# First output projection: 16 modulation tiles from PE products to VectorE row sums; row transfers of the second input projection spread over more weight units

## The reference

```python
s_lat, s_ctx = silu(c), silu(c_ctx)
for l in range(2):                                   # first block
    shift, scale, gate = split(s_lat @ w_mod[l] + b_mod[l], 3)
    shift_c, scale_c, gate_c = split(s_ctx @ w_mod[l] + b_mod[l], 3)
    hx = rmsnorm(x, norm_g[l]) * (1 + scale) + shift       # 256 x 2048
    hc = rmsnorm(ctx, norm_g[l]) * (1 + scale_c) + shift_c
    y, y_c = mix(hx @ w_in[l], hc @ w_in[l], ...)          # attention, pooling, convolution
    if l == 0:
        ctx = ctx + gate_c * (y_c @ w_out[l])
    x = x + gate * (y @ w_out[l])
x = rmsnorm(x, final_g)
mod = silu(c_2) @ w_mod_2 + b_mod_2                  # second block, six parts
...
```

## Time and profile before

| | us |
|---|---|
| runs before, median of 3 | 3036.22 |
| lowest, highest | 3032.48, 3045.45 |
| the profiled execution | 3027.13 |
| its span, first to last instruction | 3025.4 |
| PE busy | 2879.7 (95%) |
| POOL busy | 1828.3 (60%) |
| DVE busy | 1689.8 (56%) |
| ACT busy | 1455.1 (48%) |
| transfers | 620.46 MB, 205 GB/s on average |

### The profile page before, as it was taken

The page is one execution under the profiler, slowest core; times in us unless marked ns, Lnnn a source line. Parts: engine busy times, 40 slices in busy tenths (PEclk is TensorE's granted clock), DMA queues, the critical chain, the costliest instruction groups (busy, mean ns, idle before and its releaser), DMA issues.

```text
span 3025.4 us, 49352 instructions
## 1 busy us (share of the span) xinstructions
PE 2879.7 (95%) x18353; PEld 2486.3 (82%) x18353; DVE 1689.8 (56%) x2879; ACT 1455.1 (48%) x2231; POOL 1828.3 (60%) x756
## 2 busy tenths in 40 slices
PE   7799999999889989999997999999999999999999
PEld 5688886777768888878877888899987888888888
DVE  2477972899533668247669999673324444442000
ACT  3222223556422432248645777675445555555443
POOL 1244443333233565445575677677887888888998
PEclk9999999999999999999998999999999999999999
DMA  9877322555676695233593444444555666765665
GB/s 397 320 264 274 137 97 97 184 193 202 256 271 244 249 396 230 97 105 112 183 348 130 151 154 152 147 147 159 186 191 173 239 238 223 245 215 193 206 208 187
DMA packets 148917, 620.46 MB, mean 205 GB/s; under 512 B 16512, under 2 KB 17840, under 8 KB 129840
## 3 DMA queue, kind: packets, MB, share of 16 engines
q1 hardware_dynamic: 147632, 613.44, 57.0%
q10 hardware_dynamic: 1152, 5.24, 0.5%
HBM read 616.49 MB, written 2.12 MB: 204 GB/s over the span
## 4 chain that ended last, share of the span: by engine, by line
issue 46%; POOL 29%; PE 23%; POOLq 1%; DVE 0%; DVEq 0%
POOL w_low L690 29%; PE bank L725 16%; PE bank L726 8%; POOLq L685 0%; POOLq L689 0%; POOLq L690 0%; DVE region L1866 0%; DVE region L1869 0%; DVEq L1866 0%; POOLq L2675 0%
## 5 line engine op out<-in xcount | busy, mean ns | idle before, releaser
L690 POOL TENSOR_TENSOR w_low<-raw,w_high 128x1024 fp32r<-128x1024 f32 x752 | 1828.1, 2448 | 1186.5 <-ACT w_high L1224 1182.6
L1224 ACT ACTIVATE w_high<-raw 128x1024 fp32r<-128x1024 f32 x752 | 792.9, 1057 | 836.6 <-PE bank L738 410.2
L736 PE MATMUL bank<-h,w_high 128*128 128x256 f32 (+1 forms) x2816 | 951.8, 338 | 18.4 <-POOL w_low L690 15.2
L738 PE MATMUL bank<-h,w_low 128*128 128x256 f32 (+1 forms) x2816 | 935.6, 332 | 0.0
L737 PE MATMUL bank<-h,w_high 128*128 128x256 f32 (+1 forms) x2816 | 935.6, 332 | 0.0
L736 PEld LDWEIGHTS bank<-h,w_high 128*128 128x128 f32 x2816 | 537.7, 191 | 98.9 <-issue 28.6
L725 PE MATMUL bank<-h,w_high 128*128 128x512 f32 x1664 | 584.9, 397 | 9.6 <-POOL w_low L690 4.8
L738 PEld LDWEIGHTS bank<-h,w_low 128*128 128x128 f32 x2816 | 537.4, 191 | 51.0
L737 PEld LDWEIGHTS bank<-h,w_high 128*128 128x128 f32 x2816 | 538.0, 191 | 49.8 <-issue 0.7
L726 PE MATMUL bank<-h,w_low 128*128 128x256 f32 x1664 | 464.3, 279 | 0.0
L725 PEld LDWEIGHTS bank<-h,w_high 128*128 128x128 f32 x1664 | 314.9, 189 | 85.3 <-POOL w_low L690 6.1
(11 more groups left out here) (258 smaller groups left out, 3484.9 us busy)
## 6 DMA issues: line engine op xcount, KB each, us to landing
raw<-in_w_in SPq DMA_DIRECT2D x344, 512.0 KB, 3.7
raw<-in_w_up SPq DMA_DIRECT2D x176, 512.0 KB, 3.8
region<-in_w_rows SPq DMA_DIRECT2D x55, 1024.0 KB, 7.7
raw<-in_w_out SPq DMA_DIRECT2D x96, 512.0 KB, 6.0
raw<-in_w_down SPq DMA_DIRECT2D x96, 512.0 KB, 3.6
region<-in_w_mods SPq DMA_DIRECT2D x44, 1024.0 KB, 7.9
row_extra<-in_w_half_rows SPq DMA_DIRECT2D x86, 512.0 KB, 4.4
row_extra<-in_w_rows SPq DMA_DIRECT2D x41, 1024.0 KB, 7.6
```

The source lines that it names most:

```text
L690: nc.gpsimd.tensor_tensor(WL[s][:, part], RAW[s][:, part], WH[s][:, part], ALU.subtract) \
L736: nc.tensor.matmul(bank[:, 0:n], WH[slot][:, w], h, start=first and j == 0, stop=False)
L738: end = nc.tensor.matmul(bank[:, 0:n], WL[slot][:, w], h, start=False, stop=last and j == len(blocks) - 1)
L1224: return nc.scalar.activation(out, in_, func, **kw)
```

## The change

The 16 tiles 48 to 63 leave PE. Their weights are laid out as rows, together with those of tiles 80 to 95, and both are computed on DVE in out0 as quarter rows: 512 columns of four output tiles make one unit of 1 MB (32 units), and in front of each quarter stands a transfer of two vectors (x and ctx). A unit of tiles 48 to 63 takes eight sums (four tiles, two vectors), a unit of tiles 80 to 95 four. Partial sums of three quarters are kept in `ROW_PART` and added at the end. There are two places, `ROW_EXTRA` and the old `BUF_OUT0`, and `ROW_OUT` takes the products of the first vector, because a second sum still needs the weights. `out0_rows(n)` says how many of the 36 rows are used after residual n; SP issues one more than that before the weights of tile n + 4. The modulation products, their copies on ACT and adds on DVE go. In in1 the `plan` is flatter, and DVE takes a row after every second tile of the context norm.

```diff
-    ROW_OUT0 = [ROW_EXTRA[:, 0:HALF], ROW_EXTRA[:, HALF:UNIT], ROW_OUT[:]]
+    ROW_OUT0 = [ROW_EXTRA[:], *r2(10240)]
+    out0_rows = lambda n: min(36, 4 + 9 * (n + 1) // 4)
...
         def row_out0(e):
-            if e % 17 == 0:
-                row_cond("out0", e, slice(0, 1), e // 17)
+            if e == 1:
+                sp.wait_ge(sem("at_y"), 8)
+            if e % 9 == 0:
+                row_cond("out0", e, slice(0, 2), e // 9, 4)
             else:
-                row_load("out0", e, dram["w_half_rows"][16 * (e // 17) + e % 17 - 1])
+                row_load("out0", e, dram["w_rows"][96 + 8 * (e // 9) + e % 9 - 1])
...
-                    begin, plan = 4, [3 + max(0, t - 5) + max(0, t - 12) for t in range(28)]
+                    begin, plan = 4, [3 + 3 * max(0, t - 4) // 4 + 7 * max(0, t - 19) // 4 for t in range(28)]
...
             if name == "w_out0":
                 two(1)
-                for e in range(3):
-                    row_out0(e)
-                sp.wait_ge(sem("at_y"), 8)
-                for t in range(16):
-                    if t:
-                        sp.wait_ge(sem("mod_mm"), M_OUT0 + t)
-                    mod_load(BUF_OUT0[0], 0, M_OUT0 + t)
-                    for e in range(3 + 2 * t, min(34, 5 + 2 * t)):
+                asked = 0
+                for t in range(4, 17):
+                    plan = out0_rows(t - 4) + 1 if t < 16 else 36
+                    for e in range(asked, plan):
                         row_out0(e)
-                    if 2 <= t < 14:
-                        one(t + 2)
+                    asked = plan
+                    if t < 16:
+                        one(t)
...
-        def residual_tiles(u0, t0_, hi, lo, t0, n, name, width, before=None, after=None):
...
+        def residual_tiles(u0, t0_, hi, lo, t0, n, name, width):
+            two_tiles(u0, t0_, hi, lo, t0, n)
+            tiles(u0, t0_, 16, hi, lo, t0, n, 1)
...
+            weights = [place[:, QUARTER * r:QUARTER * (r + 1)] for r in range(4)]
+            if unit < 4:
+                for r, c in ((0, 0), (1, 0), (0, 1), (2, 0), (1, 1), (3, 0), (2, 1), (3, 1)):
+                    if c:
+                        own.wait(1 if r < 3 else 0)
+                    last = row_sum(total(r, c), weights[r], weights[r] if c else ROW_OUT[:, QUARTER * (r % 2):QUARTER * (r % 2 + 1)],
+                                   6 + c, QUARTER)
+                    if c == 0:
+                        own.mark(last)
+            else:
+                for r in range(4):
+                    last = row_sum(total(r, 0), weights[r], weights[r], 6, QUARTER)
+            last.then_inc(sem("row_used"), 1)
...
-                    rows_in1(1 + m)
-                for e in range(17, 33):
+                    if m % 2:
+                        rows_in1(1 + m // 2)
+                for e in range(9, 33):
                     rows_in1(e)
...
-                    if s == 3:
-                        mod_add(AUX[1], Q_OUT0 + i, 48 + 4 * i)
```

More of the change, by code:

```diff
@@ L56, in tiles_of, with rows_of @@
     return w.reshape(kt, P, nt, P).transpose(2, 1, 0, 3).reshape(nt, P, kt * P)
[L59 removed]
+def rows_of(tiles, part=0, parts=1):
     rows = tiles.reshape(-1, P, KT, P).transpose(0, 3, 2, 1).reshape(-1, P, D)
[L62 to L64 removed]
+    n = D // parts
+    return rows[:, :, n * part:n * (part + 1)].reshape(-1, parts, P, n).transpose(0, 2, 1, 3).reshape(-1, P, D)
 def pairs_of(w):
@@ L96, in lay_out @@
     mods = np.concatenate([tiles_of(w) for w in (a["w_mod"][0], a["w_mod"][1], a["w_mod_2"][0])])[first]
[L97 to L102, removed]
+    out["w_mods"] = mods[:32]
+    early, late = np.concatenate([mods[32:48], mods[64:80]]), np.concatenate([mods[48:64], mods[80:96]])
+    out["w_rows"] = np.concatenate([rows_of(early, 0, 2), rows_of(early, 1, 2), rows_of(mods[96:128]),
+                                    rows_of(mods[128:144], 0, 2), rows_of(mods[128:144], 1, 2),
+                                    rows_of(mods[176:192], 0, 2), rows_of(mods[176:192], 1, 2),
+                                    *(rows_of(late, q, 4) for q in range(4))])
+    rows = rows_of(mods[144:176])
+    out["w_half_rows"] = np.concatenate([rows[:, :, :HALF], rows[:, :, HALF:]])
     order2 = list(range(24, 32)) + list(range(24)) + list(range(32, 64))
@@ L2048, in rows_out0, with total @@
         def rows_out0(e):
-            half, m = e // 17, e % 17 - 1
-            if m < 0:
-                row_vector("out0", e, 6, HALF)
+            q, unit = e // 9, e % 9 - 1
+            if unit < 0:
+                row_vector("out0", e, 6, 2 * QUARTER)
                 return
             place = row_landed("out0", e)
-            total = mod_col(80 + m, 0) if half else ROW_PART[:, m:m + 1]
-            row_sum(total, place, place, 6, HALF).then_inc(sem("row_used"), 1)
-            if e == 33:
-                row_bias(ROW_ALL["out0"], 80, 16, 0, 1, 0).then_inc(sem("row_out"), 1)
+            def total(r, c):
+                n = 4 * unit + r
+                if q == 3:
+                    return mod_col(48 + n if unit < 4 else 64 + n, c)
+                col = 48 * q + (2 * n + c if unit < 4 else 16 + n)
+                return ROW_PART[:, col:col + 1]
+            weights = [place[:, QUARTER * r:QUARTER * (r + 1)] for r in range(4)]
[11 more added lines that the diff above has]
+            last.then_inc(sem("row_used"), 1)
+            if e == 35:
+                dve.wait_ge(sem("row_used"), ROW_ALL["out0"])
+                part = [ROW_PART[:, 48 * i:48 * (i + 1)] for i in range(3)]
+                for i in (1, 2):
+                    seq(add(part[0], part[0], part[i]))
+                row_bias(ROW_ALL["out0"], 48, 16, 0, 2, 0)
+                row_bias(ROW_ALL["out0"], 80, 16, 0, 1, 32).then_inc(sem("row_out"), 1)
         def rows_in1(e):
@@ L2300, in _ @@
                 if l == 0:
-                    for e in range(4 + 2 * n, min(34, 6 + 2 * n)):
+                    for e in range(out0_rows(n - 1), out0_rows(n)):
                         rows_out0(e)
```

66 lines of the change are left out of this document (14 added, 52 removed).

## The result

The changed kernel took 3002.16 us (median of 4 runs, 2997.65 to 3006.05), the kernel before in the same comparison 3040.84 us (4 runs, 3032.48 to 3045.74). The ratio is 0.9878, 95% interval 0.9853 to 0.9904: faster, by 1.2%. Timed again in a later comparison, it stood at 0.9909 (0.9881 to 0.9937). The profiled execution has a span of 2998.6 us, 26.8 less than the one before.

The account below looks back on a forecast made before the run. PE, busy 95% of the span, was taken as the bound, with time won where its work moves or it waits. Gains of 23 us in out0 and 11 in in1 made 34, giving 3002 us; range 2987 to 3022.

Parts of the forecast that it names:

- Sums of 512: Out0, VectorE: 512-column row sums follow each other in 0.61 us, bounds 0.57 and 0.69; 192 sums make 117 us.
- Rival B: Out0: sums cost 0.69 us, a quarter 45, out0 ends near 991; gain 22 us, total 3014 us; chance 0.17.
- Loads: Out0: a 1 MB row lands 4.9 us after issue, 5.1 with semaphores; bounds 3.7 and 8.2.
- Rival C: Out0: at a load of 6.6 us a quarter takes 48.3, only in1 pays, total 3025 us; chance 0.08.
- E: Out0, quicker rival: rows land in 3.7 us, a quarter costs 39.5, total 2993 us; chance 0.08.
- Rival D: Out0: ring of two places becomes the bound, 8.2 us per load, quarter 54.7; slower, 3053 us; chance 0.03.
- at PE's own pace: Out0: the row chain takes 42.3 us a quarter against 43.5 for PE's four tiles, and keeps its starting lag.
- The lag: Start of out0: row 1 lands at 809, rows 1 to 3 take 15 us, residual 0 at 824, tile 4 6 us late.
- Residual 15: End of out0: comes at 979 instead of 1002.2, gaining 23 us, with 3 us for last rows holding in1's weights.
- In1: Second input projection: tiles at 5.76 us up to tile 20, no ScalarE wait on the context norm; 11 us gained.
- Rival F: In1: the new plan does nothing or moves the stall to tile 12's wait; total 3013 us; chance 0.07.
- The tile's cost on PE: Out0: a tile without modulation work takes 10.88 us; a modulation tile costs PE 1.25, its summing up 1.3.

Follow-up runs that it names:

- third place: Changed kernel with a third place for out0's rows from row 14 and rows asked one further ahead from tile 9; timed 3002.68 us, ratio 0.9868.
- weights early: Changed kernel with in1's first two weight units loaded before rows 33 and 34 instead of behind row 35; 3009.62 us, ratio 0.9859.
- in1 alone: Kernel before with only in1's new row plan and row sums at every second context norm tile; 3021.99 us, ratio 0.9927.
- the squares first: Changed kernel with ScalarE's squares of tiles 13 and 14 put ahead of the high parts of in1's first two weight units; 3009.79 us.
- sums in PSUM: Changed kernel with partial sums and bias gathered in a free PSUM bank after rows 8, 17 and 26; 2994.88 us in a single execution.

## Why the prediction was right, and where it was not

**The direction, the time and the range** held: forecast 3002 us within 2987 to 3022, measured 3002.16. Much of that closeness is luck. The sum was 34 us; by the stages it is 30.0, and the two timed comparisons gave 38.7 and 28.3, ten apart for the same pair of kernels.

**Sums of 512.** Taken as 0.61 us between the bounds 0.57 and 0.69; they start 0.61 to 0.62 apart. Rival B, which took the duration (0.68) for the distance, is out. The quarter was 42.3 by the sum and came out as 43.2 and 42.7.

**Loads.** Taken as 5.1 us, of which 4.9 were the load; the medians are 5.4 and 5.6, at 303 GB/s where 301 was forecast. The mechanism (a pair of rows costs one load plus one sum) holds, since a third place took 3.3 us from a quarter. Rival C's 6.6 and E's 3.7 were not reached. Rival D named the right resource, with a price (8.2) that didn't come. The forecast that the ring runs "at PE's own pace" and keeps its lag was right: 43.2 and 42.7 us a quarter against 43.5 for PE's four tiles, with residual 14 at 168.7 us after the vector copy. It had no term for making that lag up; the third place did so and took 11.6 us from out0. The fit of the Trainium skill that the prediction cites (DMA: Bandwidth & Descriptors, the anatomy of one DMA; 4.4 us) is given there for transfers issued from GpSimd, and these are issued by SyncE.

**The lag.** Row 1's sums began 4.2 us after the vector copy (7.6 forecast, 809 against 801.4), residual 0 came at 23.4 (22.6), and tile 4 waited 6.5 us for its weights (6). That residual 0 fits is luck: row 1 was 3.4 us sooner than forecast, and rows 1 to 3 took 19.2 us instead of 15, because row 2, issued at 805.28 us, landed only at 817.63 and VectorE waited 4.5 us for it. The sum had no term for that wait. PE ended at 171.2 (169.1); some 1.5 of the 2.1 us is the granted clock of 0.51 behind its gap, for which there was no term either.

**Residual 15, the step that failed.** It was put at 979, which is 177.6 us after the vector copy; it came at 183.0. Row 35's sums ended at 177.9, so all up to there was right, the hold by in1's weights included (taken as 3 us; 5.2 of wait were seen). What was left out is the tail behind them: two additions of partial sums and the bias, 5.0 us. The prediction counted the sums and not the instructions that the added table of three quarters needs. Their plain price is 1.2 us, as weights early showed; the rest, 3.9, is GpSimd's low parts. The kernel before had no 128x48 addition, but its 128x16 one of 2.30 us beside a low part showed that price. With it out0 gave 18.1 us instead of 23.

**In1.** 11 us forecast, 11.9 measured. Evictions go 5.76 us apart from 1067.37 to 1101.93, and ScalarE no longer waits for the context norm. The convolution went later as said, and its cover fell from 52.38 to 20.07 us (28 forecast) and was not used up: the rows ended 56.1 us after tile 20's start, where the forecast had some 50. Rival F is out, in1 alone being the proof.

**The tile's cost on PE** was not tested by itself: no run left out the modulation tiles alone. The pace fits, though: 11.02 us a tile over the twelve, against the forecast's 10.88, with some 1.5 us in all lost at the clock of 0.51.

## What to carry to other kernels

When work moves to VectorE, list every instruction that it needs, the small ones at the end of the chain too, and look at what GpSimd does at that moment: an addition of 48 columns with both inputs in SBUF cost up to 2.3 us on the critical path, and one of the same shape with an input in PSUM took 0.22. A ring of places that runs at the bound's own pace never makes up a lag, so give it a place more or start it sooner. Where two engines wait for a third in turn, taking one wait away can give nothing until the next is gone: the squares first moved VectorE 4.8 us ahead and residual 15 by 0.4, since the time saved was waited out behind GpSimd.

## What the hardware showed that was not expected

VectorE gets one two-input SBUF addition through per GpSimd instruction when those follow each other without a pause: four additions in a row took 4.64 (two), 2.25 and 2.27 us beside four low parts of 2.31, and GpSimd's own time did not grow (9.24 us for four, against 9.29 in sums in PSUM, where VectorE waited for none of them). The row sums, with one operand in PSUM, kept 0.68 us beside the same work (the sums of 978.49 to 979.78 in weights early, beside the low part of 978.59).

The same instructions after in1 took 1882.7 to 1886.1 us in six profiled executions and 1895.5 to 1902.7 in the other seven of the table, with a granted clock of 0.978 to 0.983 in all. The difference arises in the last 740 us, evenly: the second execution of the changed kernel is 2.5 us behind the first at 2277 us and 15.8 at 2985. PE has no gap there in either, and the granted clock is 1.00. The windows view of 2300 to 2950 us, first execution and second:

```profile
2300.00:2950.00 650.00, 650.00 (x3752) 573.13 (x3751) 201.50 (x421) 346.44 (x488) 574.79 (x242) 1.00 0.65 221
```

```profile
2300.00:2950.00 650.00, 650.00 (x3681) 563.65 (x3681) 201.92 (x422) 341.70 (x484) 561.95 (x238) 1.00 0.64 217
```

PE does 3752 matmuls in one and 3681 in the other, 173 and 177 ns each. The other executions divide the same way: 3745 to 3753 in the six, 3681 or 3682 in the seven. What sets the two levels stays open. A different mix of them can explain why medians of a few executions were up to 15 us off the sum of the stages; that was not tested. It is why the stages were compared instead.
